# A two-block transformer kernel: end of the mixing stage in another order, zeros written midway, output tails by halves, RWKV state evacuations earlier

## The reference, cut to what matters

```
# block 1, two layers
for layer in (0, 1):
    h = x @ w_in                        # main | memory query | gates
    y_main = causal_multiscale_pool(h_main)         # layer 0
    y_main = forgetting_attention(h_main, k, v, cum) # layer 1: 16 heads, softmax of
                                        # q.k/8 + cum[t] - cum[s], causal
    y_mem = softmax(q k_mem^T) v_mem    # 4 heads, 256 memory tokens
    y = concat(y_main * silu(g_main), y_mem * silu(g_mem)) @ w_out
    x = layer_norm(ALPHA * x + y)
# block 2
h = rmsnorm(x) * (1 + scale1) + shift1 ;  z = h @ w_in_2
y_a = gmlp(z[:, :1024])                 # u * (tril(ws) @ layer_norm(v))
y_b = rwkv7(z[:, 1024:])                # a state recurrence over the sequence, 8 heads:
    # S = S*w + (S a) b^T + v k^T ;  y = S r
x = x + gate1 * (concat(y_a, y_b) @ w_out_2)
h = rmsnorm(x) * (1 + scale2) + shift2
x = x + gate2 * moe(h)                  # 4 groups x 8 experts, top 2, blocks of 128 rows
out = rmsnorm(x)
```

## Time and profile before

| what | before |
|---|---|
| median of three runs | 3078.43 us (3071.15 to 3080.0) |
| profiled execution | 3087.37 us, span 3085.6 us |
| mean granted clock of TensorE | 0.97 |
| busy: PE, DVE, ACT, POOL | 2895.9 (94%), 1779.8 (58%), 1094.2 (35%), 454.5 (15%) |
| DMA | 454.44 MB, mean 147 GB/s |

### The profile page before, as it was taken

How to read it: one execution, slowest core, us unless ns; L and a number is a source line. 1 busy time by engine, 2 the same in 40 slices (tenths; PEclk the granted TensorE clock), 3 DMA queues, 4 the chain that set the end, 5 groups by cost and what they waited for, 6 DMA issues and landing times. The chain is left out here.

```text
span 3085.6 us, 47695 instructions
## 1 busy us (share of the span) xinstructions
PE 2895.9 (94%) x19486; PEld 2179.9 (71%) x19486; DVE 1779.8 (58%) x2743; ACT 1094.2 (35%) x1700; POOL 454.5 (15%) x352
## 2 busy tenths in 40 slices
PE   8999999999999999989999999998898999999991
PEld 6877644676777777767747768687688777777760
DVE  3332222485566666555434626253874899999984
ACT  2111100122455454452231313222531566665652
POOL 2222100021322222213131101010000000000001
PEclk9999999999999999999999999998898999999995
DMA  4111031663222112121221211016346899999975
GB/s 167 45 38 45 15 129 55 184 194 123 61 61 63 55 55 62 56 100 51 68 56 34 65 29 60 7 59 202 129 166 224 329 396 397 398 398 398 397 286 231
DMA packets 290940, 454.44 MB, mean 147 GB/s; under 512 B 15760, under 2 KB 157584, under 8 KB 290752
## 3 DMA queue, kind: packets, MB, share of 16 engines
q1 hardware_dynamic: 283696, 426.06, 39.6%
q0 software_dynamic: 7056, 25.69, 2.1%
HBM read 389.77 MB, written 61.93 MB: 146 GB/s over the span
## 5 line engine op out<-in xcount | busy, mean ns | idle before, releaser
L1016 PE MATMUL psum<-x_hi,w_hi 128*128 128x512 f32 x512 | 210.6, 411 | 2.3 <-PEq L100 1.6
L1207 DVE TENSOR_TENSOR fox_pT_lo<-psum,fox_pT_hi 128x512 fp32r<-128x512 f32 (+2 forms) x192 | 107.1, 558 | 180.7 <-ACT fox_pT_hi L1146 171.6
L1018 PE MATMUL psum<-x_hi,w_lo 128*128 128x512 f32 x512 | 201.0, 393 | 0.0
L1017 PE MATMUL psum<-x_lo,w_hi 128*128 128x512 f32 x512 | 199.9, 390 | 0.0
L3065 ACT CAST hi_d<-land_d 128x2048 fp32r<-128x2048 f32 x66 | 122.8, 1909 | 141.0 <-PE psum L2935 141.0
L721 PE MATMUL psum<-wo,yT 128*128 128x512 f32 x384 | 167.6, 593 | 2.9 <-PEq L100 1.5
L1704 PE MATMUL psum<-hT,wr 128*128 128x512 f32 x384 | 167.1, 593 | 0.0
L3120 DVE TENSOR_TENSOR lo_d<-land_d,hi_d 128x2048 fp32r<-128x2048 f32 x66 | 148.3, 2289 | 21.5 <-ACT hi_d L3065 21.5
L3120 DVE TENSOR_TENSOR lo_g<-land_g,hi_g 128x2048 fp32r<-128x2048 f32 x66 | 150.6, 2283 | 0.1
L1157 ACT ACTIVATE fox_p<-fox_p,fox_bias 128x256 f32<-128x256 f32 (+7 forms) x128 | 99.6, 778 | 118.5 <-DVE fox_bias L1193 114.9
L180 PE MATMUL psum<-x_lo,w_hi 128*128 128x512 f32 x352 | 138.3, 393 | 0.0
(11 more groups left out here) (526 smaller groups left out, 7049.2 us busy)
## 6 DMA issues: line engine op xcount, KB each, us to landing
land_g<-in_moe_w_gate SPq DMA_DIRECT2D x66, 1024.0 KB, 7.9
land_u<-in_moe_w_up SPq DMA_DIRECT2D x66, 1024.0 KB, 8.9
land_d<-in_moe_w_down SPq DMA_DIRECT2D x66, 1024.0 KB, 9.4
ada<-in_ada_w SPq DMA_DIRECT2D x24, 1024.0 KB, 5.6
y_slots<-yb SPq DMA_DIRECT2D x33, 512.0 KB, 10.3
w<-in_w_in SPq DMA_DIRECT2D x27, 512.0 KB, 3.9
w_land<-in_w_kv_shared SPq DMA_DIRECT2D x23, 512.0 KB, 4.1
w_land<-in_w_in SPq DMA_DIRECT2D x23, 512.0 KB, 3.9
```

Source lines behind the costliest of these rows:

```text
L1016: nc.tensor.matmul(bank[:], hi[:, d, :], E.x_hi[:, d, cols], start=(d == 0), stop=False)
L1017: nc.tensor.matmul(bank[:], hi[:, d, :], E.x_lo[:, d, cols], start=False, stop=False)
L1018: last = nc.tensor.matmul(bank[:], lo[:, d, :], E.x_hi[:, d, cols], start=False, stop=(d == ND - 1))
```

## The change

- The two w0 loads go from the constants stage to the start of SyncE's program in the next stage.
- Output stages: for the last tile (t = 7) all chunks of half 0 come ahead of all chunks of half 1.
- Memory heads: 6 fillers between the scores and the transposes of the last head.
- fox: 6 fillers ahead of `turn` in step 62 and 12 in step 63.
- rwkv_pairs: DVE's evacuation of MT and N is a function `states(c)`, run for c < 3 inside `sums(c+1)`, ahead of the wait for `exp2`; PE's 10 fillers ahead of Q go.
- mix: in turn 11 the router's products of tile 6 and 9 fillers come ahead of the turn of tile 7; DVE evacuates the second half of tile 7's h2T (`last_rows_half`) while ACT does the first; the 8 + 18 fillers at the end become 4. The zeros go out in 6 parts of 128 x 10 x 256 in the turns 2 to 7, where they went in 5 of 128 x 12 x 256 in 8 to 12.
- experts: 16 fillers in place of 7 ahead of the second table.

```diff
@@ constants: SyncE @@
-                win = A["w_in"][0].rearrange("(c p) n -> p c n", p=P)
-                for i in range(2):
-                    col = (2 * (len(POOL_WINDOWS) - 1) + i) * P
-                    sp.dma_start(E.w0[i], win[:, :, col:col + P]).then_inc(E.w0_landed[i], 16)
@@ memory keys and values: a SyncE program with these lines @@
+            @block.sync
+            def _(sp):
...
@@ NormTurn @@
-    def evacuate(self, act, t):
+    def evacuate(self, act, t, halves=(0, 1)):
-        for h in range(2):
+        for h in halves:
@@ output stage: PE @@
-                    for c in range(NY):
+                    by_chunk = [(c, hf) for c in range(NY) for hf in range(2)]
+                    by_half = [(c, hf) for hf in range(2) for c in range(NY)]
+                    for c, hf in by_chunk if t < NT - 1 else by_half:
...
-                        if c == whole:
+                        if c == whole and hf == 0:
                             pe.wait_ge(y_split, t + 1)
...
-                        if layer == 1 and t == NT - 1 and c == whole - 1:
+                        if layer == 1 and t == NT - 1 and c == whole - 1 and hf == 1:
                             last.then_inc(whole_used, 1)
@@ fox: PE @@
+                    if n >= STEPS - 2:
+                        keep_warm(nc, E, pe, ringP, 6 if n < STEPS - 1 else 12)
                     turn(n, 0)
@@ memory heads: PE @@
                     if h + 1 < MEM_HEADS:
                         project(h + 1)
+                    else:
+                        keep_warm(nc, E, pe, ringD, 6)
                     attn.turn(pe, h)
@@ rwkv_pairs: PE, then DVE @@
                     fill_("N", c)
-                    if c + 1 < NPAIR:
-                        keep_warm(nc, E, pe, ringA, 10)
...
+                    if c >= 1:
+                        states(c - 1)
                     dve.wait_ge(S_["exp2"], c + 1)
...
+                def states(c):
                     V = nc.vector
                     for q in range(2):
                         dve.wait_ge(ringD.full, ringD.nth(("MT", c, q)))
                         V.tensor_tensor(chunk(MTs, q), u3(ringD.bank(("MT", c, q))),
...
+                def tail(c):
+                    V = nc.vector
+                    if c + 1 == NPAIR:
+                        states(c)
@@ mix: zeros, PE, SyncE, ACT, DVE @@
-        ZEROS = OVER * D // ZW // 5
+        ZERO_PARTS = 6
+        ZEROS = OVER * D // ZW // ZERO_PARTS
...
+                    if t == NT + 3:
+                        router(t - 5)
+                        keep_warm(nc, E, pe, ringA, 9)
                     if 4 <= t <= NT + 3:
...
-                    if 5 <= t:
+                    if 5 <= t and t != NT + 3:
                         router(t - 5)
                     out(t - 3, 1, 1)
-                    if t == NT + 3:
-                        keep_warm(nc, E, pe, ringD, 8)
-                keep_warm(nc, E, pe, ringD, 18)
+                keep_warm(nc, E, pe, ringD, 4)
...
-                    if t == NT:
+                    if t == 2:
                         sp.wait_ge(zeros_set, 1)
-                    if t >= NT:
-                        part = slice((t - NT) * ZEROS, (t - NT + 1) * ZEROS)
+                    if t < 2 + ZERO_PARTS:
+                        part = slice((t - 2) * ZEROS, (t - 1) * ZEROS)
                         sp.dma_start(further[:, part, :], ...
-                sp.wait_ge(zeroed, 16 * 5)
+                sp.wait_ge(zeroed, 16 * ZERO_PARTS)
...
-                        norm.evacuate(act, t - 4)
+                        norm.evacuate(act, t - 4, halves=(0, 1) if t < NT + 3 else (0,))
...
+                def last_rows_half():
+                    t, h = NT - 1, 1
+                    dve.wait_ge(ringA.full, ringA.nth(("t", t, h)))
+                    for k in range(4):
+                        c = 4 * h + k
+                        last = V.tensor_scalar(norm.to[:, c, t * P:(t + 1) * P], ringA.bank(("t", t, h))[:, k * P:(k + 1) * P],
+                                               norm.scale[:, c:c + 1], norm.shift[:, c:c + 1], ALU.mult, ALU.add)
+                    last.then_inc(ringA.free, 1)
...
+                    if t == NT + 3:
+                        last_rows_half()
@@ experts: PE @@
-                        keep_busy(7 if k else 44)
+                        keep_busy(16 if k else 44)
```

More of the change, by code:

```diff
@@ L320, in _ @@
                     nc.scalar.copy(E.mv[:, m, :], ring.bank(("v", m))[:])
+            @block.sync
+            def _(sp):
+                win = A["w_in"][0].rearrange("(c p) n -> p c n", p=P)
+                for i in range(2):
+                    col = (2 * (len(POOL_WINDOWS) - 1) + i) * P
+                    sp.dma_start(E.w0[i], win[:, :, col:col + P]).then_inc(E.w0_landed[i], 16)
             @block.gpsimd
@@ L714, in _ @@
                             pe.wait_ge(wo_split, c - whole + 1)
[L715 removed]
+                        if c == whole and hf == 0:
                             pe.wait_ge(y_split, t + 1)
[L717 to L729 removed]
+                        cols = slice(hf * HALF, (hf + 1) * HALF)
+                        if c < whole:
+                            rows = E.wo_first[c][:, cols] if layer == 0 and c < 2 else wo[:, c, cols]
+                            last = nc.tensor.matmul(banks[hf][:], E.yT[:, c, t * P:(t + 1) * P], rows, start=first, stop=final)
+                        else:
+                            hi, w_hi = y_hi[t % 2][:, c - whole, :], wo_hi[:, c - whole, cols]
+                            nc.tensor.matmul(banks[hf][:], hi, w_hi, start=first, stop=False)
+                            nc.tensor.matmul(banks[hf][:], hi, wo_lo[:, c, cols], start=False, stop=False)
+                            last = nc.tensor.matmul(banks[hf][:], E.y_lo[:, c, t * P:(t + 1) * P], w_hi, start=False, stop=final)
+                        if final:
+                            last.then_inc(ringD.full, 1)
+                        if layer == 1 and t == NT - 1 and c == whole - 1 and hf == 1:
                             last.then_inc(whole_used, 1)
@@ L2214, in level @@
                         V.tensor_tensor(XT[:, j, :], XT[:, j, :], ringD.bank(key)[:], ALU.add).then_inc(ringD.free, 1)
[L2216 removed]
+                chunk = lambda to, q: to.rearrange("p (t q n) -> p t q n", q=2, n=HD)[:, :, q, :]
+                u3 = lambda x: x.rearrange("p (t n) -> p t n", n=HD)
+                def states(c):
                     V = nc.vector
[L2218 to L2219 removed]
                     for q in range(2):
```

15 lines of the change are left out of this document (removed).

## The result

| | before | after |
|---|---|---|
| median | 3080.0 us (3071.15 to 3081.94, 5 runs) | 3053.58 us (3052.85 to 3057.41, 5 runs) |
| ratio | | 0.9923, 95% interval 0.9907 to 0.9939 |
| profiled execution, span | 3087.37, 3085.6 us | 3053.29, 3051.5 us |
| mean granted clock | 0.97 | 0.977 |

The kernel became 26.4 us faster by the medians (0.8%; the interval of the ratio is about 19 to 29 us). 33.6 were forecast, to 3045; the time lies in the range. The two traces differ by 34.1, which looks like the sum of the terms, but is not: the trace of before is an execution 7 us above its own median, that of after one at its median. So I look at the stages.

A forecast was written before the change was run, and what follows sets the result against it. TensorE, busy 94%, bounds the kernel, so only its waits or half-clock time can be won. Terms sum to 33.6: 3087.4 becomes 3053.8, less 9.0 for the median 3044.8, written 3045; range 3034 to 3063.

The forecast's parts named there:

- rival 2: RWKV: delayed DVE operations or bank order make PE wait, the 7.2 goes; gain 26.4, time 3052; chance 0.1.
- RWKV: RWKV stage: state additions run sooner, so PE's next product starts 2.41 earlier for three pairs; gain 7.2.
- Only behind idle PE stretches of 2 us and more: Granted clock: in the trace it fell only behind such PE idle stretches (2.26, 3.83, 4.19).
- First loads: First stage: w0 loads moved over the barrier let PE start the second stage at about 21.95; gain 2.85.
- Tile halves: Output stages, last tile: half 0's addition, 1.45, leaves the path; gain 1.45 in the first, 1.1 in the second.
- Memory head: Last memory head: six fillers before the transposes keep the clock up for transposes and values; gain 3.0.
- Attention: Last two attention turns (fox): fillers keep full clock for scores and turn; gain 4.2, at most 4.8.
- End of mixing: End of mixing: router moved ahead, evacuation split, fewer fillers; next stage sooner by 13.3, or 10.1 if the clock falls.
- Zeros: Mixing: zeros sent between stream loads cost 0; bound 42, each of six parts exposed whole at 7.0.
- Rival 3: Mixing: zeros hold up the stream loads, 42 lost against 33.6 won, time 3087; decides from 5.6 a part; chance 0.03.
- Experts: Experts, second table: 16 fillers keep the products at full clock; gain 0.5, or a loss of up to 4.
- Rival 1: Clock falls in spite of the fillers; gain 22.7, time 3056, or 3062 with further losses; chance 0.2.

The follow-up runs named there:

- more_fillers: The changed kernel with 6 fillers in layer 0's last memory head, 3, 15 and 4 in fox, 6 before mixing's last router; 3051.36 us, ratio 0.9904.
- three_undone: The changed kernel with w0 loads back in the first stage, last tile by chunks, 7 fillers before the second table; 3062.3 us, ratio 0.9939.
- no_fillers: The changed kernel without the fillers in the last memory head and fox and the 9 in mixing; 3063.66 us, ratio 0.9956.
- zeros_at_once: The changed kernel with all six parts of zeros issued in turn 2, not one each in turns 2 to 7; 3058.39 us, ratio 0.9927.
- rwkv_undone: The changed kernel with the RWKV stage as before; 3067.1 us, ratio 0.9954.
- fillers_only: The kernel before with only the 24 fillers of the memory and fox edits; 3080.06 us, ratio 0.9997.
- rwkv_and_fillers: The kernel before with the RWKV edit and the 24 memory and fox fillers; 3065.14 us, ratio 0.9956.
- rwkv_only: The kernel before with only the RWKV edit: state evacuations ahead of the next pair's two long operations, ten fillers gone; 3078.0 us, ratio 0.9995.

## Why the prediction was right, and which terms were off

The direction, the range and most of the mechanisms were right; the size was 7 too large. It is chance that the 26.4 is the very gain of rival 2, whose mechanism did not come. Point by point:

- **The sum and the offset.** Trace to trace the kernels differ by 34.1, and that this fits the sum of 33.6 is luck. Some 7 of it lie where the change does nothing: half clock in layer 0 (1.9) and at the start of out 1 (1.5), and mostly waits for weights in the memory stage (3.4). What is left in this pair of traces is 27.4, close to the 26.4 of the medians. So the terms were too large by 6: the end of mixing by 2.0, the experts by 2.3, fox by 1.4, the tile halves by 1.0, RWKV by 0.9, while the first loads won 1.7 more than I had. In the last step of the sum I then took off the 9.0 between trace and median as if they lay in both kernels alike; the trace of after lies at its median.
- **What the clock falls behind.** "Only behind idle PE stretches of 2 us and more" was misread already in the trace of before: it also fell behind 1.80 in layer 0's last memory head, where the values took 5.85 in place of 3.70. That idle time is the same (1.80) in 13 of the 14 traces, all but more_fillers, and half clock stands behind it in 4, as the free-running monitor of the Trainium skill (TensorE: Matmul & The Clock Gate, Part 1) would have it.

```profile
374.43 3.33 PE L373 MATMUL psum<-ident,mem_probs 128*128 128x128 f32 x16 [1.80 <-DVE mem_probs L406]
378.44 5.85 PE L384 MATMUL psum<-mem_probsT,mv 128*128 128x512 f32 x8 [0.68 <-ACT mem_probsT L436]
```

- **First loads** (2.85): 3.07 in the first stage, and 1.4 to 2.8 more behind it, since behind an idle time of 4.24 to 4.73 the clock was low in the second stage in seven traces of seven, and behind 1.54 to 1.78 in none of seven. Shown by three_undone: 5.7. I had named this as a bound (1.5).
- **Tile halves** (1.45 and 1.1): 0.65 and 0.78 by three_undone. I read the distance of the two additions, 1.45, as what one half costs behind the last product. But in the old order half 0's bank is full one product earlier, and its addition started at 564.00, while the last product still ran (TensorE turns tile 6 from 564.58 on); only part of the 1.45 was on the path. In after the one addition left starts 0.27 behind TensorE's turn of tile 6 (558.08, 558.35), in before the second one started 0.87 behind the same turn (565.45):

```profile
564.58 1.04 PE L698 MATMUL psum<-ident,x_tile 128*128 128x128 f32 x8
```

- **Memory head** (3.0): from the scores' end to the next stage 13.5 to 13.8 in four traces with half clock and without the fillers, 11.1 in all nine with them, and 11.1 in no_fillers, where the clock held: 2.4 to 2.7 or nothing. The rest of that stage's 6.1 are mostly two waits for weights (1.64 and 1.41 in before). Of the other traces only zeros_at_once has both (1.47 and 1.56), a kernel with the edit, so they come and go from execution to execution.
- **Attention** (4.2): 2.8 from trace to trace, 3.5 against no_fillers. The fillers saved the scores' clock; it fell half a turn later, behind two idle times of a microsecond, in five of the seven traces with these fillers. Those seven take 612.4 to 613.8, the five without 615.4 to 617.1.
- **RWKV** (7.2): 2.4 three times, as worked out, and no turn was late (rival 2 falls). What I did not see is TensorE's instruction supply. With the count of the kernel before, the edit was worth 1 to 2; with 24 fillers ahead of it 13.3 (rwkv_undone less after). From before to after, where the fillers come too, it came to 6.3.
- **End of mixing** (13.3, or 10.1 at half clock): 11.6 from trace to trace, 8.0 against the draw of 16.0 that three of five unedited traces show; and 1.3 more were lost in the experts' first fillers, which ran at half clock in after. The term was sized from the heavier draw.
- **Zeros** (0): 0. The loads behind a part landed 3.4 later (medians 4.0 and 7.4), which is 1.31 MB at 0.39 MB per us, not the 7.0 of the part's own landing. The rule of the Trainium skill (DMA: Bandwidth & Descriptors, Queues, rings and completion order) that descriptors of a ring are consumed in order agrees with this and doesn't conflict with zeros_at_once; the price that I had joined to it was twice too high. Rival 3 needs more than 5.6 a part.
- **Experts** (0.5): 0. The table's products took 1.98 in place of 3.48, but VectorE's next operation (L3120, two in 4.50) held the gather's indices as before, and TensorE then waited 3.02 for the gathered rows. With its start at half clock the stage lost 1.8.
- **Rival 1**, the clock falls all the same, came true in part: in fox, at the last router, and in the experts' start.

That the RWKV stalls stand where the number of TensorE instructions ahead puts them is shown for the places: six kernels with the edit and 24 fillers have them at 108 to 109, 216 to 218 and 353 to 355, the two with none at 206 to 208, 304 to 308 and 344 to 348, and the two without the edit and with 24 at 232 to 233, 372 and 511 to 513; two of these groups were foretold. The Trainium skill (Runtime: NRT & Kernel Launch, Instruction fetch mechanics) says that an engine's instructions come in blocks of a fixed size, fetched by a transfer of the sequencer's own while the block before is executed, and that the crossing is mostly hidden. The places agree with the first part. As to the second, the stage has 64 or 65 such transfers and 2 to 6 stalls over 0.4 in a trace: most crossings are hidden, and the others cost up to 1.7 in the dense stretches of 64 x 64 products and 3.0 at 354.

The traces show the transfers themselves, as packets of 16 KiB on the queue q8 (`instruction`) of the DMA view (in after 140 packets with 2.29 MB). In the RWKV stages of the 14 traces TensorE has 45 idle times over 0.4 that end by "issue", and every one of them ends 2.2 to 2.8 behind the start of such a packet, while the packets are 3.2 or more apart. That ties the stalls to the instruction supply more directly than their places do. It also tells what makes the stall at 354 long: where it is 1.3, the packet starts 1.25 ahead of the stall; where it is 2.8 to 3.0, it starts 0.3 to 0.4 behind the stall's start. Here are the packet of after (window 1878.3:1878.8) with the stall that it ends, and the same of three_undone (window 1887.7:1888.2):

```profile
q8 instruction: 1, 0.02, 11.0%
1881.04 1.32 PE L1760 MATMUL psum<-w_uv,hT 128*128 128x256 f32 x5 [1.28 <-issue]
```
```profile
q8 instruction: 1, 0.02, 11.0%
1890.50 1.79 PE L1757 MATMUL psum<-w_uv,hT 128*128 128x256 f32 x4 [3.02 <-issue]
```

Busy data queues are not the common cause. In the 1.5 us ahead of the packet the DMA engines were over 90% busy at 27 of the 45 stalls, but at most 27% at the other 18, the three of 1.7 in fillers_only among them. At 354 they were full in the long and in the short cases alike.

Not settled: why the packet at 354 comes late in four of six executions, and how the 26.4 split over the stages beyond what one trace of each kernel gives.

## What to carry to other kernels

Take two or three traces of the kernel before you size a gain of tenths of a per cent: a term read from a stretch at half clock is the size of one draw, and the trace's distance from the median hints at the side on which it errs. Look first for filler and idle time that ends a stage: it gave about half of this gain (the end of mixing, fox and the memory head), while the careful reordering of VectorE's work gave 7.2 that TensorE's instruction supply could take away or nearly double. Where TensorE runs dense streams of small products, a few instructions added anywhere ahead move the stalls, so an edit's worth is measured in place, with the rest of the change, and not alone.

## What the runs showed of the hardware

- TensorE stalled for its own instructions for 0.5 to 3.0 us at places that moved with the number of instructions ahead; 24 fillers (48 records) ahead of an untouched stage made it 9 to 10 us longer (fillers_only against before) or 3 us shorter (rwkv_and_fillers against rwkv_only).
- Each of 45 such stalls ended 2.2 to 2.8 us behind the start of an instruction packet (16 KiB, q8), and the longest ones were those where the packet started only after the stall had begun.
- The same idle time of 1.80 in layer 0 was followed by half clock in 4 of 13 traces, that of 2.25 in the memory stage in 4 of 5, and that of 4.24 to 4.73 ahead of the second stage in 7 of 7.
- SyncE's issue of six transfers of 1.31 MB in a row took 17.40 us, and what stood behind them on its queue was issued after that. One such transfer ahead of a load of `n` moved the median of its landing from 4.0 to 7.4 us.
